# A decoder layer on one core: a pair of value units in 512 columns, the last product in two column halves, and an opening with x in quarters

## Chip, core, metric

The kernel runs on one core of a Trainium2 chip. The metric is device microseconds of one execution. The engines are PE (TensorE: matmuls, with PEld its weight loads), ACT (ScalarE), DVE (VectorE), POOL (GpSimd) and SP, whose queue issues nearly every DMA.

## What is computed

One decoder layer on 256 tokens of width 1024 with a memory of 256 tokens, and a final RMSNorm, all in float32. RWKV-7 has 8 heads of 64, attention 8 heads of 64, cross attention 4 heads of 256.

```python
def reference(x, mem, ...):
    u = rms_norm(h, norm_mix[l]); z = u @ w_in[l]
    y_rwkv = rwkv7_time_mix(z[..., :RWKV_IN], ...)
    y_moba = moba_attention(q, k, v)
    h = h + jnp.concatenate([y_rwkv, y_moba], axis=-1) @ w_mix_out[l]
    h = h + memory_cross_attention(rms_norm(h, ...), rms_norm(mem, ...), w_xq[l], w_xkv[l], w_xo[l])
    a = jnp.square(jax.nn.relu(rms_norm(h, norm_ffn[l]) @ w_ff1[l]))
    h = h + a @ w_ff2[l]
    return rms_norm(h, norm_final)
```

## The kernel before

**Units, halves, quarters.** All dense products are cut into units of 1 MB of weights (`UNITS`). In their order these are seven `z` (input projection of RWKV, units 0 to 6), four `mq` and two `mv` (queries, keys and values of the attention), four `xk` and three `xv` (keys and values of the memory, units 13 to 19), four `mix`, the last `xv`, four `xq`, four `xo`, then `f1` and `f2` (the MLP). SP loads unit u into one of three buffers of `raw`, once the unit three before it has been split. A unit has two halves `s`; `hi(s)` on ACT (L1081) rounds a half of `raw` into `w_hi`, `lo(s)` on DVE (L1589) writes the rest into `w_lo`, and PE multiplies hi by hi, hi by lo and lo by hi. The matmuls of a half come in two quarters, in the order of `QUARTERS`; a quarter has 12 matmuls of 256 columns, or 6 of 512. `dense(n)` in PE's program runs the next n quarters, in the text called q0, q1, ...

**Results.** `take(o)` on DVE scales output o out of a bank and counts `out_taken`. PE begins output o only when o-2 has been taken, since two banks (`dense_bank`) alternate. An `xv` unit gives 256 columns of the value matrix for both token halves, side by side in one bank: L465 to L467.

**The order** of each engine's program is written out by hand, as lists of calls such as `dense(2)`, `spread(0)`, `take(3)`. There is no scheduler. What waits, waits in that order.

**The opening.** SP loads the row `norm_mix`, then x in two halves of 512 columns (`x_in`) alternating with the halves of unit 0 (`first_in`), then 12 small parameter rows (L332), and unit 1. PE turns x, 256 columns per `load(0, q)` (L579, four transposes). ACT scales that into `op_hi` (L1133) and DVE makes `op_lo` (L1697). `copies` (L1705) keeps x for the residual. `stats(0)` on ACT (L1146) sums the squares of x for the norm, `diagonal_of(0)` on DVE makes a diagonal of it, and `spread(0)` on PE (L590) spreads it over a bank, from which `spread_copy` takes it. `params(1)` turns the parameter rows on PE (L562) and copies them on DVE (L1680 to L1684); `spread(0)` writes the bank from which that copy reads, and so waits for its end (`dve_params`).

**The middle.** `lora()` (L616) needs `gates()` of ACT. Then `rates()` on ACT, the scan `sums()` on DVE, `key_sums()`, `key_norm()`, `keys()`, and `tokens()` on PE (L663), which needs DVE's last product of the key chain (L1788).

**The end.** The last `f2` unit (columns 512 to 1023) runs token half 0, then token half 1, each as 12 matmuls of 512 columns. `finish()` takes four pieces, (token half, column half) = (0,0), (1,0), (0,1), (1,1). DVE adds the residual (L1996) and multiplies the gain (L1999). ACT sums the squares (L1298). After a token half's second piece come a root on ACT (L1304), a reciprocal on DVE (L2005), and the scaling by it, half of the columns on ACT (L1309) and half on DVE (L2008). SP then issues two stores per token half (L348).

## Time and profile before

| | |
|---|---|
| three timed runs | 471.09, 471.23, 471.69 us, median 471.23 |
| the profiled execution, its own time | 471.15 us |
| its span, first to last instruction | 469.3 us |
| busy share of PE, DVE, ACT, POOL | 97%, 69%, 50%, 7% |
| the chain that ended last, share on PE | 92% |

The profiled execution's own time lies 1.85 us over its span; what is found in the trace is a part of the span. The chain that ended last is followed back from the last instruction. As long as it stands on PE, only PE's own work sets the time.

### The profile page before, as it was taken

To read this page: it belongs to the slowest core of one execution; us is meant where nothing else is said; L and a number is where in the kernel's file an instruction comes from. 1 tells how busy PE (TensorE), PEld (TensorE's weight loads), DVE (VectorE), ACT (ScalarE), POOL (GpSimd) and SP (SyncE) were. 2 spreads that over 40 slices of the span, in tenths; PEclk is the share of its full clock that TensorE was granted. 3 is DMA by queue.
4 is the path that set the end of the run, shared out by engine and by line. 5 is a ranking of instruction groups with operands and counts; after the bars stand their busy time and mean duration, and the time that the engine had idled before them with its cause. 6 is when DMAs were issued, how large, how long until landed. Compare 5 with 4: busy or idle time off the path is not lost.

```text
span 469.3 us, 10580 instructions
## 1 busy us (share of the span) xinstructions
PE 454.7 (97%) x4518; PEld 413.7 (88%) x4518; DVE 323.6 (69%) x491; ACT 236.8 (50%) x373; POOL 34.8 (7%) x50
## 2 busy tenths in 40 slices
PE   5999999989999999999999999999999999999994
PEld 4999999979898899999998898888888888888883
DVE  4778999897576477668766368866555756574745
ACT  5789843343354226436444455545465546354534
POOL 8100000000000000071000001340000000000000
PEclk9999999999999999999999999999999999999999
DMA  7973534505060522462552166655656565856502
GB/s 255 336 239 94 180 112 157 185 9 176 3 205 5 178 92 91 134 226 91 180 179 91 33 189 189 218 180 180 180 153 207 186 199 163 260 181 217 184 0 91
DMA packets 61410, 73.07 MB, mean 156 GB/s; under 512 B 1314, under 2 KB 51572, under 8 KB 61364
## 3 DMA queue, kind: packets, MB, share of 16 engines
q1 hardware_dynamic: 61284, 72.14, 48.5%
q8 instruction: 36, 0.59, 0.5%
q0 software_dynamic: 80, 0.26, 0.2%
q14 instruction: 10, 0.08, 0.1%
HBM read 71.35 MB, written 1.05 MB: 154 GB/s over the span
## 4 chain that ended last, share of the span: by engine, by line
PE 92%; DVE 4%; DMA 1%; ACT 1%; issue 1%; SPq 0%; ACTq 0%
PE bank L497 13%; PE bank L512 11%; PE bank L513 10%; PE bank L514 10%; PE bank L529 6%; PE bank L531 6%; PE bank L530 6%; PE bank L499 6%; PE bank L465 2%; PE bank L466 2%; PE bank L467 2%; PE bank L881 2%; PE bank L905 1%; DMA xval<-in_x 1%; PE bank L641 1%; PE bank L496 1%
## 5 line engine op out<-in xcount | busy, mean ns | idle before, releaser
L1589 DVE TENSOR_TENSOR w_lo<-raw,w_hi 128x1024 fp32r<-128x1024 f32 x130 | 160.4, 1241 | 67.4 <-ACT w_hi L1081 67.1
L1081 ACT ACTIVATE w_hi<-raw 128x1024 fp32r<-128x1024 f32 x130 | 136.8, 1057 | 111.3 <-PE bank L514 52.0
L497 PE MATMUL bank<-op,w_hi 128*128 128x512 f32 x256 | 89.1, 398 | 0.0
L512 PE MATMUL bank<-op,w_hi 128*128 128x256 f32 x288 | 83.7, 291 | 0.1
L513 PE MATMUL bank<-op,w_hi 128*128 128x256 f32 x288 | 81.4, 283 | 0.1
L514 PE MATMUL bank<-op,w_lo 128*128 128x256 f32 x288 | 81.4, 283 | 0.0
L499 PE MATMUL bank<-op,w_lo 128*128 128x256 f32 x224 | 62.8, 281 | 0.0
L512 PEld LDWEIGHTS bank<-op,w_hi 128*128 128x128 f32 x288 | 55.1, 191 | 1.2 <-issue 0.8
L513 PEld LDWEIGHTS bank<-op,w_hi 128*128 128x128 f32 x288 | 55.2, 192 | 0.2
L514 PEld LDWEIGHTS bank<-op,w_lo 128*128 128x128 f32 x288 | 55.1, 191 | 0.2 <-issue 0.2
L497 PEld LDWEIGHTS bank<-op,w_hi 128*128 128x128 f32 x256 | 46.4, 188 | 8.8
L529 PE MATMUL bank<-w_hi,op_hi 128*128 128x512 f32 x128 | 50.0, 390 | 0.0
L531 PE MATMUL bank<-w_hi,op_lo 128*128 128x512 f32 x128 | 49.8, 389 | 0.0
L530 PE MATMUL bank<-w_lo,op_hi 128*128 128x512 f32 x128 | 49.8, 389 | 0.0
L499 PEld LDWEIGHTS bank<-op,w_lo 128*128 128x128 f32 x224 | 42.3, 189 | 1.3
L512 PE MATMUL bank<-op_hi,w_hi 128*128 128x256 f32 x128 | 37.9, 296 | 0.7 <-DVE op_lo L1984 0.7
L513 PE MATMUL bank<-op_lo,w_hi 128*128 128x256 f32 x128 | 36.2, 283 | 0.0
L514 PE MATMUL bank<-op_hi,w_lo 128*128 128x256 f32 x128 | 36.1, 282 | 0.0
L1114 ACT ACTIVATE tmp<-bank 128x256 f32<-128x256 f32 x32 | 12.3, 384 | 37.6 <-PE bank L497 37.5
L531 PEld LDWEIGHTS bank<-w_hi,op_lo 128*128 128x128 f32 x128 | 24.0, 188 | 5.1
L530 PEld LDWEIGHTS bank<-w_lo,op_hi 128*128 128x128 f32 x128 | 24.0, 188 | 5.0
L529 PEld LDWEIGHTS bank<-w_hi,op_hi 128*128 128x128 f32 x128 | 24.0, 188 | 4.7
(268 smaller groups left out, 732.1 us busy)
## 6 DMA issues: line engine op xcount, KB each, us to landing
raw<-in_w_ff SPq DMA_DIRECT2D x32, 1024.0 KB, 5.3
raw<-in_w_in SPq DMA_DIRECT2D x12, 1024.0 KB, 6.0
raw<-in_w_xkv SPq DMA_DIRECT2D x8, 1024.0 KB, 5.6
raw<-in_w_mix_out SPq DMA_DIRECT2D x4, 1024.0 KB, 5.1
raw<-in_w_xq SPq DMA_DIRECT2D x4, 1024.0 KB, 5.2
raw<-in_w_xo SPq DMA_DIRECT2D x4, 1024.0 KB, 5.4
xval<-in_x SPq DMA_DIRECT2D x2, 512.0 KB, 4.4
raw<-in_w_in SPq DMA_DIRECT2D x2, 512.0 KB, 5.4
```

The lines of the kernel that those rows point to most:

```text
L465: mm(dst, hi, wh[:, k, :], start=(xk == 0), stop=False)
L497: last = mm(b[:, :], wh[:, k, :], op_both[0][:, :, k, :], start=first, stop=final)
L499: mm(b[:, 0:T], wl[:, k, :], op_hi[0][:, k, :], start=False, stop=False)
L512: mm(dst, wh[:, k, :], op_hi[which][:, k, :], start=first, stop=False)
L513: mm(dst, wh[:, k, :], op_lo[which][:, k, :], start=False, stop=False)
L514: last = mm(dst, wl[:, k, :], op_hi[which][:, k, :], start=False, stop=final)
L529: mm(dst[:, :], hi, wh[:, k, :], start=first, stop=False)
L530: mm(dst[:, :], hi, wl[:, k, :], start=False, stop=False)
L531: last = mm(dst[:, :], lo, wh[:, k, :], start=False, stop=final)
L1081: op(view(w_hi), r, ACT.Copy).then_inc(hi_done, 1)
L1114: op(tmp[:, n % 2, T * half:T * half + T], half_bank(s)[:, T:2 * T], ACT.Copy).then_inc(act_part, 1)
L1589: tt(view(w_lo), r, view(w_hi).bitcast(f32), ALU.subtract).then_inc(lo_done, 1)
```

## The change

1. **Values in 512 columns.** Units 17 and 18 (`xv` 0 and 1) become one product of 512 columns: unit 17 holds input rows 0 to 511, unit 18 rows 512 to 1023, of the same 512 columns. Token half 0 goes to one bank, token half 1 to the other, which `o = 16` has to leave first; so `take(16)` stands earlier in DVE's list (before `state(3)`), and `take(17)` later (behind `pair_scores(3)`).
2. **The end.** For token half 1 the last unit is done in columns 512 to 767, then 768 to 1023, into another bank (`dense_bank[0]`). `finish()` has five pieces, and token half 1 is scaled 384 columns on ACT and 640 on DVE; ACT issues the store of its own part.
3. **The opening.** x comes in quarters, the second one ahead of unit 0's first half. `norm_mix` is issued by ACT. Unit 1 is issued ahead of the 12 parameter rows. PE runs transposes of `ident` into an unused bank (`warm`, 4 and 7 of them). The lists of calls are in another order.

```diff
-    out += [("xv", "w_xkv", 0, D + 256 * j, j) for j in range(3)]
+    out += [("xv", "w_xkv", 4 * j, D, j) for j in range(2)]
+    out += [("xv", "w_xkv", 0, D + 256 * j, j) for j in range(2, 3)]
     out += [("mix", "w_mix_out", 0, 256 * j, j) for j in range(4)]
...
+def wide_of(u):
+
+    what, _, _, _, j = UNITS[u]
+    return  what == "xv" and j < 2
...
                      ((0, 0), (2, 0), (0, 1), (1, 0), (1, 1), (2, 1), (3, 0), (3, 1))]
+    elif wide_of(_u) and UNITS[_u][4] % 2 == 0:
+
```
```diff
         gain_out, hid_sq = flat(s0[:, :, :]), flat(s3[:, :, :]).rearrange("p (n c) -> p n c", n=2)
-        fin = sb("fin", [128, 10])
-        r_sq, sq_sum, first_sum, root = fin[:, 0:2], fin[:, 2:6], fin[:, 6:8], fin[:, 8:10]
+        fin = sb("fin", [128, 12])
+        r_sq, sq_sum, first_sum, root = fin[:, 0:2], fin[:, 2:7], fin[:, 7:10], fin[:, 10:12]
+        PIECES = [(0, 0, 512), (1, 0, 512), (0, 512, 512), (1, 512, 256), (1, 768, 256)]
+        SIDE = [512, 384]
 
         bank = [ctx.enter_context(nc.psum_tensor(f"bank{i}", [128, 512], f32)) for i in range(8)]
...
             for half in range(2):
-                c, k = slice(512 * half, 512 * half + 512), slice(4 * half, 4 * half + 4)
-                sp.dma_start(stage[0][:, :, c], x[:, :, c]).then_inc(x_in[half], 16)
+                for q in (2 * half, 2 * half + 1):
+                    c = slice(256 * q, 256 * q + 256)
+                    sp.dma_start(stage[0][:, :, c], x[:, :, c]).then_inc(x_in[q], 16)
+                k = slice(4 * half, 4 * half + 4)
                 sp.dma_start(first_to[:, k, :], first[:, k, UNITS[0][3]:UNITS[0][3] + 256]).then_inc(first_in[half], 16)
...
-                k, n = (4, 512) if what == "f2" else (8, 256)
+                k, n = (4, 512) if what == "f2" or wide_of(u) else (8, 256)
                 sp.dma_start(raw[:, u % NRAW, :].rearrange("p (k c) -> p k c", k=k),
                              w[:, r:r + k, c:c + n]).then_inc(raw_in[u % NRAW], 16)
 
+            load_unit(1)
...
-            load_unit(1)
...
-            for n in range(NT):
-                for j, done in enumerate((act_final, dve_final)):
-                    c = slice(512 * j, 512 * j + 512)
-                    sp.wait_ge(done, n + 1)
-                    sp.dma_start(o[:, n, c], ostage[:, n, c]).then_inc(out_done, 16)
+            for n, done, c in ((0, act_final, slice(0, SIDE[0])), (0, dve_final, slice(SIDE[0], D)),
+                               (1, dve_final, slice(SIDE[1], D))):
+                sp.wait_ge(done, n + 1)
+                sp.dma_start(o[:, n, c], ostage[:, n, c]).then_inc(out_done, 16)
```
```diff
+                if wide_of(s // 2):
+                    j = UNITS[s // 2][4] % 2
+                    o -= j
+                    if j == 0 and q == BEGUN[s] + 1 and s == OUTS[o][1]:
+                        pe.wait_ge(out_taken, o)
+                    for k in range(2):
+                        xk = 4 * j + 2 * (s % 2) + k
+                        hi, lo = op_hi[which][:, xk, tokens_of(part)], op_lo[which][:, xk, tokens_of(part)]
+                        dst = dense_bank[(o + part) % 2][:, :]
+                        mm(dst, hi, wh[:, k, :], start=(xk == 0), stop=False)
+                        mm(dst, hi, wl[:, k, :], start=False, stop=False)
+                        last = mm(dst, lo, wh[:, k, :], start=False, stop=(xk == KT - 1))
+                    if q == DONE[s]:
+                        last.then_inc(dense_mm, 1)
+                    elif j and s % 2:
+                        last.then_inc(wide_mm, 1)
+                    return
                 if what in ("mv", "xv"):
 
...
                 dst = out_acc[n][j // 2]
+                if s // 2 == len(UNITS) - 1 and n == 1:
+                    c = slice(256 * i, 256 * i + 256)
+                    to = dense_bank[0][:, 0:256] if i else dst[:, c]
+                    if i == 1:
+                        pe.wait_ge(dve_add, 2 * len(KIND["f1"]))
+                    for k in range(4):
+                        xk = 4 * (g % 2) + k
+                        _, view = split_views(s - i + k // 2)
+                        hi, lo = op_hi[1][:, xk, tokens_of(n)], op_lo[1][:, xk, tokens_of(n)]
+                        mm(to, hi, view(w_hi)[:, k % 2, c], start=(i == 1 and k == 0), stop=False)
+                        mm(to, hi, view(w_lo)[:, k % 2, c], start=False, stop=False)
+                        last = mm(to, lo, view(w_hi)[:, k % 2, c], start=False, stop=(k == 3))
+                    last.then_inc(pe_acc, 1)
+                    return
                 for k in range(2):
                     xk = 4 * (g % 2) + 2 * i + k
```
```diff
+            def warm(n):
+
+                for _ in range(n):
+                    turn_op(dense_bank[1][:, 0:128], ident[:, :], ident[:, :])
+
...
-                    pe.wait_ge(x_in[q // 2], 16)
+                    pe.wait_ge(x_in[q], 16)
...
             params(0)
+            warm(4)
             load(0, 0)
             load(0, 1)
+            warm(7)
             load(0, 2)
             load(0, 3)
+            dense(3)
+            params(1)
+            dense(1)
+            spread(0)
+            dense(9)
+            lora()
+            dense(5)
+            key_sums()
+            dense(1)
+            spread(1)
+            dense(1)
+            keys(0)
+            dense(3)
+            load(1, 0)
             dense(2)
-            params(1)
-            dense(2)
-            spread(0)
-            dense(10)
-            lora()
-            dense(2)
-            spread(1)
-            dense(2)
-            key_sums()
-            dense(2)
-            keys(0)
-            dense(2)
-            load(1, 0)
             load(1, 1)
-            dense(12)
+            dense(9)
             tokens()
...
+            def opening():
+                act.dma_start(prow[0:8, :], io["norm_mix"].rearrange("l (r p) -> (l r) p", p=128)).then_inc(mix_in, 16)
+                act.wait_ge(pool_const, 1)
+                op(small[:, 15:16], eps[:, 0:1], ACT.Sqrt)
```
```diff
                     act.wait_ge(dve_hinv, n + 1)
                     act.wait_ge(dve_hgain, n + 1)
-                    out_half = ostage[:, n, 0:512]
-                    op(out_half, out_half, ACT.Copy, scale=root[:, n:n + 1]).then_inc(act_final, 1)
-
+                    out_part = ostage[:, n, 0:SIDE[n]]
+                    op(out_part, out_part, ACT.Copy, scale=root[:, n:n + 1]).then_inc(act_final, 1)
+                act.wait_ge(act_final, 2)
+                act.dma_start(out.rearrange("b (n p) d -> p (b n) d", p=128)[:, 1, 0:SIDE[1]],
+                              ostage[:, 1, 0:SIDE[1]]).then_inc(out_done, 16)
+
+            opening()
             load(0, 0)
             load(0, 1)
```
```diff
+                if wide_of(OUTS[o][0]):
+                    if j % 2:
+                        dve.wait_ge(dense_mm, OUTS[o][2] + 1)
+                    else:
+                        dve.wait_ge(wide_mm, wide_no(o))
+                    values_of, m = (mval, 0) if what == "mv" else (xval, 1)
+                    n = j % 2
+                    ts(values_of[:, n, 512 * (j // 2):512 * (j // 2) + 512], dense_bank[o % 2][:, :],
+                       row_sum[:, 2 * m + n:2 * m + n + 1], None, ALU.mult).then_inc(out_taken, 1)
+                    return
                 dve.wait_ge(dense_mm, OUTS[o][2] + 1)
...
                     dve.wait_ge(pe_acc, i + 1)
-                    h = h_tok[:, n, c]
-                    stt(out=h, in0=out_acc[n][j][:, :], scalar=r_sq[:, n:n + 1], in1=h, op0=ALU.mult, op1=ALU.add)\
-                        .then_inc(dve_h, 1)
+                    h = h_tok[:, n, c:c + 512] if c < 768 else h_tok[:, n, 768:D]
+                    src = out_acc[n][c // 512][:, :] if c < 768 else dense_bank[0][:, 0:256]
+                    stt(out=h, in0=src, scalar=r_sq[:, n:n + 1], in1=h, op0=ALU.mult, op1=ALU.add).then_inc(dve_h, 1)
+                    h = h_tok[:, n, c:c + size]
                     dve.wait_ge(dve_h, i + 1)
-                    tt(ostage[:, n, c], h, gain_out[:, c], ALU.mult).then_inc(dve_hgain, 1)
-                    if j == 0:
+                    tt(ostage[:, n, c:c + size], h, gain_out[:, c:c + size], ALU.mult).then_inc(dve_hgain, 1)
+                    if c + size < D:
                         dve.wait_ge(act_hsum, i + 1)
-                        ts(first_sum[:, n:n + 1], sq_sum[:, i:i + 1], 1.0 / D, NORM_EPS, ALU.mult, ALU.add).then_inc(dve_hsum, 1)
+                        if c:
+                            dve.wait_ge(dve_hsum, 2)
+                        ts(first_sum[:, (0, 1, 0, 2)[i]:(0, 1, 0, 2)[i] + 1], sq_sum[:, i:i + 1], 1.0 / D,
```

The rest of DVE's list up to `take(5)`, after, reads: `copies(0)`, `copies(1)`, `take(0)`, `lo(4)`, `follow(0)`, `take(1)`, `lo(5)`, `lo(6)`, `follow(1)`, `take(2)`, `diagonal_of(1)`, `lo(7)`, `follow(2)`, `lo(8)`, `sums()`, `take(3)`, `lo(9)`, `key_norm()`, `follow(3)`, `lo(10)`, `key_root()`, `lo(11)`, `spread_copy(1)`, `take(4)`, `keys(0)`, `lo(12)`, `follow(4)`, `keys(1)`, `lo(13)`, `take(5)`.

**PE, the opening.** PE's first instructions of before, with the semaphores that each waits for in brackets (`xval` holds x here, `op` the split x, `w_hi` the rounded weights):

```order
1 L558 MATMUL bank<-ident,prob 128x8 [waits mix_in,pool_const]
2 L579 MATMUL bank<-ident,xval 128x128 [waits x_in0]
3 L579 MATMUL bank<-ident,xval 128x128 x3
4 L579 MATMUL bank<-ident,xval 128x128 [waits x_in0]
5 L579 MATMUL bank<-ident,xval 128x128 x3
6 L579 MATMUL bank<-ident,xval 128x128 [waits x_in1]
7 L579 MATMUL bank<-ident,xval 128x128 x3
8 L579 MATMUL bank<-ident,xval 128x128 [waits x_in1]
9 L579 MATMUL bank<-ident,xval 128x128 x3
10 L478 MATMUL bank<-op,w_hi 128x256 [waits dve_op,hi_done]
```

And of the changed kernel, in its own line numbers; L618 is `warm`, L635 `load(0, q)`:

```order
1 L609 MATMUL bank<-ident,prob 128x8 [waits mix_in,pool_const]
2 L618 MATMUL bank<-ident 128x128 x4
3 L635 MATMUL bank<-ident,xval 128x128 [waits x_in0]
4 L635 MATMUL bank<-ident,xval 128x128 x3
5 L635 MATMUL bank<-ident,xval 128x128 [waits x_in1]
6 L635 MATMUL bank<-ident,xval 128x128 x3
7 L618 MATMUL bank<-ident 128x128 x7
8 L635 MATMUL bank<-ident,xval 128x128 [waits x_in2]
9 L635 MATMUL bank<-ident,xval 128x128 x3
10 L635 MATMUL bank<-ident,xval 128x128 [waits x_in3]
11 L635 MATMUL bank<-ident,xval 128x128 x3
12 L515 MATMUL bank<-op,w_hi 128x256 [waits dve_op,hi_done]
```

The turning of x waits for four loads instead of two, and 11 transposes of `ident` stand ahead of and in it.

**DVE, the opening.** From `lo(1)` to `spread_copy(0)` before; `w_lo` with `hi_done` is `lo`, the three rows from `par<-bank` on are `params(1)`:

```order
12 L1589 TENSOR_TENSOR w_lo<-raw,w_hi 128x1024 [waits hi_done]
13 L1711 RECIPROCAL row_sum<-row_sum 128x2 [waits act_root]
14 L1713 TENSOR_SCALAR prob<-ident,row_sum 128x128 [waits dve_link]
15 L1713 TENSOR_SCALAR prob<-ident,row_sum 128x128
16 L1680 COPY par<-bank 128x74 [waits pe_params]
17 L1682 TENSOR_SCALAR onemu<-par 128x14 [waits dve_link]
18 L1684 TENSOR_SCALAR one_k_a<-par 128x4
19 L1589 TENSOR_TENSOR w_lo<-raw,w_hi 128x1024 [waits hi_done,dve_params]
20 L1589 TENSOR_TENSOR w_lo<-raw,w_hi 128x1024 [waits hi_done]
21 L1718 COPY rinv<-bank 128x256 [waits pe_spread_rms]
```

And after:

```order
11 L1654 TENSOR_TENSOR w_lo<-raw,w_hi 128x1024 [waits hi_done]
12 L1786 RECIPROCAL row_sum<-row_sum 128x2 [waits act_root]
13 L1788 TENSOR_SCALAR prob<-ident,row_sum 128x128 [waits dve_link]
14 L1788 TENSOR_SCALAR prob<-ident,row_sum 128x128
15 L1654 TENSOR_TENSOR w_lo<-raw,w_hi 128x1024 [waits hi_done]
16 L1755 COPY par<-bank 128x74 [waits pe_params]
17 L1757 TENSOR_SCALAR onemu<-par 128x14 [waits dve_link]
18 L1759 TENSOR_SCALAR one_k_a<-par 128x4
19 L1654 TENSOR_TENSOR w_lo<-raw,w_hi 128x1024 [waits hi_done,dve_params]
20 L1793 COPY rinv<-bank 128x256 [waits pe_spread_rms]
21 L1780 COPY hT<-bank 128x512 [waits act_op] x4
```

`lo(2)` now stands ahead of `params(1)`, and one `lo` behind it.

**DVE, the end.** The second piece of token half 0 and the end of the program, before (L1996 residual, L1999 gain, L2005 reciprocal, L2008 scaling):

```order
425 L1996 SCALAR_TENSOR_TENSOR xval<-bank,fin,xval 128x512 [waits pe_acc]
426 L1999 TENSOR_TENSOR xkey<-xval,s 128x512 [waits dve_h]
427 L2005 RECIPROCAL fin<-fin 128x1 [waits act_hroot]
428 L2008 TENSOR_SCALAR xkey<-xkey,fin 128x512 [waits dve_hgain,dve_hinv]
429 L1996 SCALAR_TENSOR_TENSOR xval<-bank,fin,xval 128x512 [waits pe_acc]
430 L1999 TENSOR_TENSOR xkey<-xval,s 128x512 [waits dve_h]
431 L2005 RECIPROCAL fin<-fin 128x1 [waits act_hroot]
432 L2008 TENSOR_SCALAR xkey<-xkey,fin 128x512 [waits dve_hgain,dve_hinv]
```

After; L2071 is the residual, L2074 the gain, L2079 the sum of the earlier pieces' squares, L2086 the scaling:

```order
422 L2071 SCALAR_TENSOR_TENSOR xval<-bank,fin,xval 128x512 [waits pe_acc]
423 L2074 TENSOR_TENSOR xkey<-xval,s 128x512 [waits dve_h]
424 L2083 RECIPROCAL fin<-fin 128x1 [waits act_hroot]
425 L2086 TENSOR_SCALAR xkey<-xkey,fin 128x512 [waits dve_hgain,dve_hinv]
426 L2071 SCALAR_TENSOR_TENSOR xval<-bank,fin,xval 128x512 [waits pe_acc]
427 L2074 TENSOR_TENSOR xkey<-xval,s 128x256 [waits dve_h]
428 L2079 TENSOR_SCALAR fin<-fin 128x1 [waits dve_hsum,act_hsum]
429 L2071 SCALAR_TENSOR_TENSOR xval<-bank,fin,xval 128x256 [waits pe_acc]
430 L2074 TENSOR_TENSOR xkey<-xval,s 128x256 [waits dve_h]
431 L2083 RECIPROCAL fin<-fin 128x1 [waits act_hroot]
432 L2086 TENSOR_SCALAR xkey<-xkey,fin 128x640 [waits dve_hgain,dve_hinv]
```

Behind the scaling of token half 0 there are now two pieces, with three more instructions between them, where there was one.

## Rows read from the trace of the kernel before

**Rows 1.** The page: the span, and the chain that ended last by engine.
```profile
span 469.3 us, 10580 instructions
...
PE 92%; DVE 4%; DMA 1%; ACT 1%; issue 1%; SPq 0%; ACTq 0%
```

**Rows 2.** The chain of waits, 0 to 18 us: start us, us, what.
```profile
7.67 1.97 PE bank L579 x8
...
10.71 0.21 PE bank L479
...
11.09 0.12 PE bank L479
...
16.11 0.44 PE bank L590 x4
...
16.62 0.36 PE bank L512
```

**Rows 3.** The timeline, 0 to 32 us: start, duration, engine, line, [idle before <- releaser].
```profile
0.80 0.40 SPq L307 DMA_DIRECT2D prob<-in_norm_mix  x1
...
1.26 0.42 SPq L313 DMA_DIRECT2D xval<-in_x  x1
...
5.86 1.69 ACT L1133 ACTIVATE op<-bank,par 128x256 fp32r<-128x256 f32 x4 [3.56 <-PE bank L579]
...
7.44 1.06 ACT L1081 ACTIVATE w_hi<-raw 128x1024 fp32r<-128x1024 f32 x1
...
8.83 1.69 ACT L1133 ACTIVATE op<-bank,par 128x256 fp32r<-128x256 f32 x4 [0.33 <-PE bank L579]
...
14.65 0.22 DVE L1680 COPY par<-bank 128x74 f32<-128x74 f32 x1
...
15.25 2.36 DVE L1589 TENSOR_TENSOR w_lo<-raw,w_hi 128x1024 fp32r<-128x1024 f32 x2
```

**Rows 4.** The two loads of x, by tile.
```profile
DMA to landing us min/median/max: 3.4/4.4/5.4
```

**Rows 5.** The timeline of DVE, 52 to 67 us.
```profile
52.78 0.69 DVE L1633 TENSOR_TENSOR tmp<-bank,rinv 128x512 f32<-128x512 f32 x1 [0.45 <-PE bank L514]
...
65.56 1.22 DVE L1788 TENSOR_TENSOR s<-s,pend 128x1024 f32<-128x1024 f32 x1
```

**Rows 6.** The chain of waits, 66 to 80 us.
```profile
67.14 1.75 PE bank L663 x16
```

**Rows 7.** The timeline of PE in one quarter of an `xv` unit, 256 columns.
```profile
157.53 0.28 PE L466 MATMUL bank<-w_lo,op_hi 128*128 128x256 f32 x1
...
158.72 0.28 PE L467 MATMUL bank<-w_hi,op_lo 128*128 128x256 f32 x1
```

**Rows 8.** The timeline of PE in an `f2` unit, 512 columns.
```profile
445.01 0.39 PE L531 MATMUL bank<-w_hi,op_lo 128*128 128x512 f32 x1
...
445.69 0.39 PE L531 MATMUL bank<-w_hi,op_lo 128*128 128x512 f32 x1
```

**Rows 9.** The timeline from 457 us to the end.
```profile
458.86 0.74 DVE L1996 SCALAR_TENSOR_TENSOR xval<-bank,fin,xval 128x512 f32<-128x512 f32 x1
...
460.46 0.74 DVE L1996 SCALAR_TENSOR_TENSOR xval<-bank,fin,xval 128x512 f32<-128x512 f32 x1
...
462.52 0.49 DVE L2008 TENSOR_SCALAR xkey<-xkey,fin 128x512 f32<-128x512 f32 x1
...
465.18 0.72 ACT L1309 ACTIVATE xkey<-xkey,fin 128x512 f32<-128x512 f32 x1 [0.23 <-DVE fin L2005]
```

**Rows 10.** The timeline of SP's queue, the last issues.
```profile
465.93 0.81 SPq L348 DMA_DIRECT2D out<-xkey  x2
```

**Rows 11.** Groups of instructions by shape: count, busy us, mean ns of one.
```profile
L1091 ACT ACTIVATE zT<-tmp,onemu 128x256 f32<-128x256 f32 x14 | 6.3, 496 | 0.3 <-DVE tmp L1631 0.3
...
L1697 DVE SCALAR_TENSOR_TENSOR op<-bank,par,op 128x256 fp32r<-128x256 f32 x8 | 3.4, 474 | 4.0 <-ACT op L1133 4.0
```

73 lines of the change are left out of this document (37 added, 36 removed).

## Prediction

> **What bounds the kernel now.** The page first: the chain that ended last stands on PE for 92% of a span of 469.3 us [rows 1]. So a part of the change counts only by what it does to PE's path, or to the head and the tail where PE is not the last to be waited for. The chain of waits shows both. At the head the transposes of x start when the second half of x lands, at 7.67. A matmul of 256 columns then takes 0.21 us of the path until 10.7 and 0.12 from 11.1 on (PE's two clock levels, 1.2 and 2.4 GHz; before the rise PE had run the transposes from 7.67 on and seven matmuls), and unit 1's first matmul, q4, starts at 16.62 [rows 2]. From there PE runs nearly without a gap. The tail starts at 463.12 with DVE's residual of the last piece and goes through ACT and DVE by turns to SP's last issues at 465.93 [rows 9, 10].
>
> A sum is made against the profiled execution, 471.15 us by its own time, 0.08 under the median of the timed runs (471.23). What a measurement can tell from no change is about 0.2%, 0.94 us.
>
> **Opening: x earlier.** `norm_mix` leaves SP's queue, so x is issued 0.46 earlier (0.80 for 1.26) [rows 3]. The two halves of x landed 3.4 and 5.4 us after their issues at 1.26 and 2.23 [rows 3, 4] (the second at 7.63), with a half of unit 0 between them. That is two transfers of 512 KB in 2.97 us, 1.48 each. By this rate the quarters land at 3.5, 4.2, 6.4 and 7.2. PE's order in the changed kernel is row, four `warm`, `load(0,0)`, `load(0,1)`, seven `warm`, `load(0,2)`. Eight transposes took 1.97 [rows 2], some 0.21 each of the path while the clock is low. `load(0,0)` starts at 3.5, `load(0,1)` ends at 5.2, and seven more `warm` hold PE until 6.7 at the low clock, 6.4 if it has risen by then.
>
> ACT started `load(0,2)` at 8.83, 1.16 after its transposes began at 7.67 [rows 2, 3]; with four fast transposes that is 0.7. So ACT starts it at 7.2 (fast; before that ACT is busy from 4.65 on with `load(0,0)`, `load(0,1)` and `hi(0)`, which took 5.86 to 8.50 before) or 7.85 (slow). Everything behind it on ACT, `load(0,3)`, `hi(1)`, `stats(0)`, `hi(2)`, stands as before, and DVE's `lo(2)` follows it. So `lo(2)` comes earlier by 1.0 to 1.6. Between the two I take 1.3. `copies(0)`, moved back on DVE, was never on this path: DVE waits for ACT here.
>
> **Opening: one call later.** Now the order on DVE. `spread(0)` on PE waits for the end of `params(1)`, and that now stands behind `lo(2)`. Before, `lo(2)` started at 15.25 and ended at 16.43 (two in 2.36) [rows 3], and `spread(0)` had run beside it; q4 could start 0.2 later. After, behind the end of `lo(2)` come 0.60 for `params(1)` (14.65 to 15.25) [rows 3], then 0.51 for `spread(0)` (16.11 to 16.62) [rows 2], and two handovers of 0.05. q4 starts at 16.43 - 1.3 + 0.60 + 0.51 + 0.1 = 16.34 instead of 16.62: a gain of **0.28**, from 0.6 gained to nothing. PE, four quarters of 12 x 0.12 from 7.7 or 8.4 on, ends q3 near 13.4 to 14.5 and then stands still; the time that the faster start gave PE is lost there, and so the clock during q0 and q1 doesn't count.
>
> The parameter rows, now behind unit 1 (1 MB, landing near 11.6), are due at q2's end, near 12. Were they up to 2 us late they would still be ahead of `lo(2)`.
>
> **Opening: the rest of the lists.** `lora()` moves one quarter ahead, `keys(0)` and `load(1,1)` likewise around single quarters; PE's work up to `tokens()` is the same. What can grow is DVE's lag. DVE waited 0.45 for PE at 52.78 (`take(5)`), and then ran without a pause to the end of L1788 at 66.78 [rows 5], while PE began `tokens()` at 67.14 [rows 6]: a slack of 0.36. In the changed list `sums()` can start some 2 us earlier against q4, but `lo(9)` has moved behind it (1.2) and DVE then waits for the head sums on PE and for `hi(12)` on ACT, which stand where they stood. I estimate that DVE reaches `take(5)` 0.4 later against q4 than before, just the slack. I take a **loss of 0.1**, between 0 and 0.5.
>
> **Values in 512 columns.** The rows show 10 matmuls of 256 columns in 1.19 us, 0.119 each [rows 7], and 3 of 512 in 0.68, 0.227 each [rows 8]. 96 matmuls of 256 become 48 of 512: 48 x (0.238 - 0.227) = **0.54 gained**, all on PE's path, which the chain holds there. The added wait, of the second wide quarter for `take(16)`, is covered: `take(16)`, of 512 columns like the residual's 0.75 [rows 9], now stands right behind unit 16's end, and a quarter of 6 x 0.227 = 1.4 and a `state` step lie between. `take(17)` has two quarters and the head sums before its bank is wanted. If a transition or a wait does cost, I give it 0.25.
>
> **The end.** The chain of the last piece does shrink. A residual of 256 columns takes 0.47 instead of 0.75 [rows 9, 11]. ACT's time falls by 0.226 for 256 columns less (0.722 at 512, 0.496 at 256) [rows 9, 11], and I take the same for the squares. So from the residual's start to the scaling's start it is 2.06 (463.12 to 465.18) - 0.27 - 0.23 = 1.56. But DVE isn't free to start it. It scales token half 0 at 462.52 for 0.49 [rows 9], so to 462.95 or 463.0, and only then comes piece four, which was ready long before. Pieces follow each other on DVE at 1.60 (458.86 to 460.46) [rows 9], since DVE waits for ACT's squares; with 256 squares 1.37. The fifth piece starts at 462.95 + 1.37 = 464.32 where the fourth started at 463.12. Its scaling starts at 464.32 + 1.56 = 465.88, 0.70 later than 465.18. The scaling is 384 columns on ACT, 0.11 shorter. The two stores are issued beside each other instead of one after the other, the second 0.4 later (0.81 for both) [rows 10]: between nothing and 0.4 of that comes back, because the same 512 KB has to move, and I take 0.15. Sum 0.70 - 0.11 - 0.15 = **0.45 lost**, from 0.2 to 0.7. PE's two column halves cost 24 x 0.119 - 12 x 0.227 = 0.14, hidden beside DVE.
>
> On the stores the Trainium skill ("DMA: Bandwidth & Descriptors", section "Issuing engines are not separate DMA queues") says that issuing from several engines only saves the sequencer's time. By it the full 0.4 of SP's second issue would come back at most, and the end would lose 0.2.
>
> **Sum:** -0.28 + 0.1 - 0.54 + 0.45 = -0.27. 471.15 - 0.27 = 470.88, so **470.9 us**, no measurable change.
>
> **Rivals.**
>
> *The clock stays low in the opening.* `warm` is all transposes, and before, the clock was still low through the eight transposes from 7.67 on and rose only after some matmuls had run [rows 2]; the trace can't tell whether transposes raise it. If they don't, `load(0,2)` starts at 6.7, `lo(2)` gains 1.0, q4 gains nothing: 471.2. Chance 0.15. The Trainium skill ("TensorE: Matmul & The Clock Gate", Part 4, PE-mode transpose) says that transposes do not count as activity for the gate; by that rule this case would be sure.
>
> *`params(1)` costs nothing,* because `lo(2)` is done well before PE gets to `spread(0)`, say if PE is late in q0 to q3. Then q4 gains up to 1.3 and the time is 469.9. Against it stands that `hi(2)` follows `stats(0)` as before. Chance 0.12.
>
> *The tail pays as meant.* If DVE took the last piece at 463.25, right behind PE's end (463.1, when DVE now starts, + 0.14), its scaling would start at 464.81, 0.37 earlier, and the end would gain 0.37 + 0.11 + 0.15 = 0.63 instead of losing 0.45: 469.8. It would need DVE to have room for piece four ahead of 463.0; the rows show it scaling token half 0 until then. Chance 0.07.
>
> *Slower: DVE falls behind.* From `take(5)` on DVE has no pause for 14 us, and every microsecond that it comes later than the slack of 0.36 stops PE at `tokens()`. For the run to be slower by more than 0.94 the lag has to be over 1.6 where I find 0.4, for instance by `gates()` or `rates()` coming late to `lora()`. With a lag of 1.8: 472.2. Chance 0.11.
>
> The forecast keeps 0.55.
>
> **Numbers.** Inside the forecast the ends of the terms are -0.6 and 0, 0 and 0.5, -0.54 and -0.3, 0.2 and 0.7: 470.2 to 472.0 if all fell together. The two fast rivals stand at 469.8 and 469.9. The range 469.8 to 471.9 leaves out the slow rival and a part of the fast ones. Faster: the two fast rivals and a little of the forecast's edge, 0.23. Slower: 0.12. Same: 0.65.
>
> **What would show it.** Opening: PE idle for about 2 us ahead of `spread(0)`, ended by DVE's `params(1)`, and q4 near 16.3. Middle: `tokens()` less than 0.5 behind its place of before against q4. Values: 48 matmuls of 512 columns at 0.227. Tail: on DVE the residual of piece four starts when token half 0's scaling ends, not when PE is done, and the last scaling starts some 2.7 after PE's last matmul instead of 2.1. I am wrong if PE doesn't wait at `spread(0)`, if the squares or the sum of squares are quicker than these rows so that DVE is free earlier, or if a new wait shows between 16 and 100 us.

## The result and the profile after

The changed kernel takes 473.16 us (median of 13 runs), the kernel before beside it 471.73 (13 runs): ratio 1.0033, interval 1.0023 to 1.0044, so 1.1 to 2.1 us slower. The forecast was 470.9, with a range of 469.8 to 471.9. All times here are of executions at full clock but one: the profiled execution of e12_warm_only below took 745.08 us at a mean granted clock of 0.56, and of its trace only the DMA rate of the opening is used.

The page of the profiled execution (473.45 us by its own time), to compare with [rows 1]:

```profile
span 471.5 us, 10538 instructions
...
PE 88%; DVE 5%; ACT 3%; DMA 1%; issue 1%; SPq 0%; DVEq 0%; ACTq 0%
```

PE's share of the chain fell from 92 to 88%: ACT (1 to 3%) and DVE (4 to 5%) took its place, and the chain of the first 19 us says where (start us, us, what):

```profile
2.86 6.77 DMA xval<-in_x
...
9.67 1.13 PE bank L635 x4
...
10.82 0.35 ACT op L1194
...
11.55 1.05 ACT w_hi L1142
12.61 1.04 ACT neu L1207 x2
...
15.06 1.05 ACT w_hi L1142
...
16.14 1.23 DVE w_lo L1654
...
17.62 0.18 DVE one_k_a L1759
...
17.93 0.68 PE bank L646 x4
18.62 0.12 PE bank L549
```

The last quarter of x, issued at 2.86, lands at 9.6. Behind it stand, as before, the transposes, ACT's `load`, `hi(1)`, the statistics and `hi(2)`, then DVE's `lo(2)` at 16.14 (15.25 in [rows 3]), and behind `lo(2)` now `params(1)` and `spread(0)`. On PE's timeline unit 1 starts at 18.37, 1.75 later than in [rows 2]. SP's queue (start, duration):

```profile
0.81 0.95 SPq L333 DMA_DIRECT2D xval<-in_x  x2
...
2.31 1.02 SPq L333 DMA_DIRECT2D xval<-in_x  x2
...
3.88 0.51 SPq L345 DMA_DIRECT2D raw<-in_w_in  x1
4.43 3.79 SPq L354 DMA_DIRECT2D prob<-in_norm_mem  x1
```

The first parameter row behind unit 1 takes 3.79 to issue; before it took 0.43. And between 3.5 and 6.5 us the DMA engines move little, though 3 MB are queued by 4.4. The windows of PE of the changed kernel (us, PE busy, granted clock, DMA share, GB/s):

```profile
3.50:6.50 3.00, 3.00 (x17) 1.00 0.71 208
...
9.50:12.50 3.00, 2.90 (x14) 0.50 1.02 323
12.50:13.00 0.50, 0.50 (x4) 0.57 0.33 106
13.00:13.50 0.50, 0.50 (x6) 1.00 0.50 109
```

and the same stretch of the kernel before:

```profile
3.50:6.50 3.00, 1.79 (x8) 1.00 1.05 382
```

The windows also show the clock: after a wait of 2.16 for x, PE is granted half its clock (1.2 GHz) from 9.5 to about 12.9, and unit 0 begins in that stretch.

Two more places. On PE's timeline there is a wait that no engine releases ("issue"):

```profile
125.12 0.43 PE L919 MATMUL bank<-probT,mval 128*64 128x256 f32 x1
125.81 0.43 PE L919 MATMUL bank<-probT,mval 128*64 128x256 f32 x2 [0.27 <-issue]
```

And the end, the timeline of DVE and ACT, to compare with [rows 9]:

```profile
464.36 0.49 DVE L2086 TENSOR_SCALAR xkey<-xkey,fin 128x512 f32<-128x512 f32 x1
464.76 0.74 DVE L2071 SCALAR_TENSOR_TENSOR xval<-bank,fin,xval 128x512 f32<-128x512 f32 x1
...
466.21 0.47 DVE L2071 SCALAR_TENSOR_TENSOR xval<-bank,fin,xval 128x256 f32<-128x256 f32 x1
...
467.79 0.61 ACT L1370 ACTIVATE xkey<-xkey,fin 128x384 f32<-128x384 f32 x1 [0.23 <-DVE fin L2083]
468.43 0.39 ACTq L1372 DMA_DIRECT2D out<-xkey  x1
```

The same step before and after gives the ledger of the two profiles. A step's place counts against the kernel before: +1.75 at unit 1's first matmul, +1.97 at `tokens()` (68.95 for 66.98), +1.70 at 121, +2.38 from 127 on (the wait at 125), +2.15 at the first wide quarter (a wait of 0.27 that the kernel before had at 148.31 is gone), +1.81 behind unit 18, +2.61 at the last scaling, +2.2 at the end of the span.

### The profile page after: what moved, and what is told of

Its sections match the earlier page's. It is cut to its first block, busy times and chain, and to the rows that moved or that the text cites. A ratio compares the mean times of both kernels' runs of the same rounds, so it can differ in the third digit from the quotient of the medians.

```text
span 471.5 us, 10538 instructions
## 1 busy us (share of the span) xinstructions
PE 456.9 (97%) x4493; PEld 413.2 (88%) x4493; DVE 324.4 (69%) x492; ACT 236.5 (50%) x375; POOL 34.7 (7%) x50
## 4 chain that ended last, share of the span: by engine, by line
PE 88%; DVE 5%; ACT 3%; DMA 1%; issue 1%; SPq 0%; DVEq 0%; ACTq 0%
PE bank L534 13%; PE bank L549 11%; PE bank L550 10%; PE bank L551 10%; PE bank L580 6%; PE bank L582 6%; PE bank L581 6%; PE bank L536 6%; PE bank L937 2%; DMA xval<-in_x 1%; PE bank L502 1%; PE bank L503 1%; PE bank L504 1%; PE bank L961 1%; PE bank L697 1%
## 5 line engine op out<-in xcount | busy, mean ns | idle before, releaser
L580 PE MATMUL bank<-w_hi,op_hi 128*128 128x512 f32 x124 | 48.4, 390 | 0.0
L582 PE MATMUL bank<-w_hi,op_lo 128*128 128x512 f32 x124 | 48.3, 389 | 0.0
L581 PE MATMUL bank<-w_lo,op_hi 128*128 128x512 f32 x124 | 48.2, 389 | 0.0
```

Of the source, the lines that this page charges most:

```text
L580: mm(dst[:, :], hi, wh[:, k, :], start=first, stop=False)
L581: mm(dst[:, :], hi, wl[:, k, :], start=False, stop=False)
L582: last = mm(dst[:, :], lo, wh[:, k, :], start=False, stop=final)
```

## The experiments

Times are medians; a ratio is against runs of the kernel before on the same chip. "q4" is the start of unit 1's first matmul on PE's timeline; "segment" is PE's time from its first value product (L919) to the first matmul of `states_out()` that reads `neu` (L872), which the expectations call the first state step; the wide values, where present, save 0.17 in it.

### The three parts apart

**e1_values_only.** Only the units, `wide_of`, the wide branch of `dense`, `take` and the order of `take(16)` and `take(17)`:

```diff
+     out += [("xv", "w_xkv", 4 * j, D, j) for j in range(2)]
```

> The kernel before, with the value pair in 512 columns alone. Theory A (the terms of the sum stand by themselves): PE's work between the first wide quarter and the end of unit 17 is 0.34 us shorter, as in the trace of the changed kernel (0.54 by the prediction), and the time is 0.3 to 0.5 us below the kernel before; unit 1's first matmul stays near 16.6. Rival B (a wait for take(16) or take(17) eats it): PE shows a gap before a wide quarter and the time is that of before or above.

471.45 us, ratio 0.9995 (0.9984 to 1.0005). By the time alone nothing is decided; in the trace the stretch of the pair, units 17 and 18, is 0.34 to 0.36 shorter (0.15 to 0.17 ahead of `states_out()`, 0.19 behind) with no wait before a wide quarter. Theory A in the trace.

**e2_end_only.** Only `PIECES`, `SIDE`, the branch for the last `f2` unit and the stores.

> The kernel before, with the end in column halves and the last store issued by ACT alone. Theory A (DVE is the bound of the tail): DVE takes the fourth piece only after scaling token half 0, the fifth 1.4 to 1.5 us later, and the last scaling starts 0.7 to 0.8 us later than before; the time is 0.35 to 0.5 us above the kernel before. Rival B (the column halves pay as meant): the last scaling starts 0.4 us earlier and the time is 0.6 us below.

472.16 us, ratio 1.0015 (1.0006 to 1.0024): 0.3 to 1.1 slower. DVE's timeline:

```profile
463.53 0.74 DVE L2014 SCALAR_TENSOR_TENSOR xval<-bank,fin,xval 128x512 f32<-128x512 f32 x1
...
464.98 0.47 DVE L2014 SCALAR_TENSOR_TENSOR xval<-bank,fin,xval 128x256 f32<-128x256 f32 x1
...
466.56 0.55 DVE L2029 TENSOR_SCALAR xkey<-xkey,fin 128x640 f32<-128x640 f32 x1
```

The fifth piece follows the fourth by 1.45. Theory A.

**e3_opening_only.** Only the four lists, the queues, quarters and `warm`.

> The kernel before, with the changed opening alone (SP, ACT, PE and DVE lists, x in quarters, unit 1 ahead of the rows). Theory A (the opening carries the whole loss): the second pair of x quarters lands near 9 and 9.6, unit 1's first matmul starts at 18.0 to 18.5, and the time is 1.3 to 1.9 us above the kernel before. Rival B (the loss of the whole comes from the interplay, or from an instruction fetch that PE meets near 125 us): the time is within 0.6 us of the kernel before.

472.59 us, ratio 1.0021 (1.0011 to 1.0031), about 1.0 slower. q4 at 18.68, and PE's wait for nothing stands at 126.29 (0.41). The three ratios add to 1.0031, the whole has 1.0033: the parts stand by themselves. The opening gives most of the loss, though less than theory A's 1.3. In this trace DVE is not on the way to q4: from the second load's transposes (8.78) to q4 the chain stands on PE alone, at the slow pace (0.21 for 256 columns) until 15.0. The same holds in e6_no_warm and e7_params_first.

### Why x lands late

**e4_unit1_behind.**

```diff
-             load_unit(1)
              for name, (r, c) in ROW.items():
...
+             load_unit(1)
```

> The changed kernel, with unit 1 issued behind the parameter rows again. Theory U (1 MB of unit 1 in front is what holds up the second pair of x quarters and SP's queue): the long issue of the first row (3.8 us) is gone, x lands as a whole by 8.0, ACT's load(0,2) starts by 8.2, unit 1's first matmul at 16.3 to 17.0, and the time is 1.2 to 1.8 us below the changed kernel. Theory Q (quarters of 256 KB are slower transfers themselves): SP's long issue is gone but x's second pair still lands at 8.7 or later, and unit 1's first matmul stays above 17.7; the time is within 0.6 us of the changed kernel.

473.43 us, ratio 1.0033 (1.0020 to 1.0046). SP's long issue is gone and x's last quarter still takes 7.0 to land. By that my first theory, U, falls. The q4 of 19.07 and the time say nothing on x, which I had overlooked: the chain to q4 starts at unit 1, issued at 8.36 and landed at 15.4, on which `hi(2)` waits:

```profile
8.36 7.05 DMA raw<-in_w_in
15.43 1.07 ACT w_hi L1142
16.53 1.23 DVE w_lo L1654
```

**e5_x_halves.**

```diff
-                for q in (2 * half, 2 * half + 1):
-                    c = slice(256 * q, 256 * q + 256)
-                    sp.dma_start(stage[0][:, :, c], x[:, :, c]).then_inc(x_in[q], 16)
+                c = slice(512 * half, 512 * half + 512)
+                sp.dma_start(stage[0][:, :, c], x[:, :, c]).then_inc(x_in[half], 16)
```

> The changed kernel, with x in two transfers of 512 columns again, unit 1 still ahead of the rows. Theory Q (quarters are the slow part): x's second half lands by 7.8, ACT's load(0,2) starts by 8.2, SP's long issue of the first row stays, and unit 1's first matmul starts at 16.3 to 17.2: 1.0 to 1.8 us below the changed kernel. Theory U (unit 1 in front is the slow part): x's second half lands at 8.7 or later, and the time is within 0.6 us of the changed kernel.

472.76 us, ratio 1.0022 (1.0011 to 1.0033). The stretch from 3.5 to 6.5 moves 357 GB/s, x is in by 8.3, q4 at 17.36: 1.0 earlier than in the changed kernel. Of that about 0.5 shows in the time, and the intervals of the two kernels overlap. Theory Q for the mechanism; the size was less than expected.

**e8_halves_unit1.** Both edits.

> The changed kernel with x in halves and unit 1 behind the rows, so that of the new opening norm_mix on ACT's queue, warm and the new lists are left. Theories U and Q both: x is in by 7.3 (the kernel before had 7.63 with an issue 0.46 later), unit 1's first matmul starts at 15.9 to 16.5, and the time is 1.4 to 2.0 us below the changed kernel, near the kernel before or up to 0.4 us below it. Rival L (the lists themselves cost): x is in by 7.3 and the time still stays 0.5 us or more above the kernel before.

472.66 us, ratio 1.0022 (1.0011 to 1.0033), q4 at 17.28. x was issued 0.42 earlier than before and is in no earlier (8.2), which neither theory had. The time is as rival L has it, so something else costs too; in this trace a wait of 0.80 for nothing stands at 125.28.

**e9_token_rows.**

```diff
-                for q in (2 * half, 2 * half + 1):
-                    c = slice(256 * q, 256 * q + 256)
-                    sp.dma_start(stage[0][:, :, c], x[:, :, c]).then_inc(x_in[q], 16)
+                c = slice(512 * half, 512 * half + 512)
+                for n in range(2):
+                    sp.dma_start(stage[0][:, n, c], x[:, n, c]).then_inc(x_in[half], 16)
```

> The changed kernel, with x in four transfers of 256 KB that are cut by tokens instead of by columns, so that each still has rows of 2 KB as the halves had (each half of the columns is waited for as a whole). Theory R (the rows of 1 KB of the column quarters are what slows the stretch from 3.5 to 6.5 us): that stretch moves 290 to 400 GB/s, x is in by 8.3, unit 1's first matmul starts near 17.3, and the time is 0.3 to 0.9 us below the changed kernel. Theory N (the number or the size of the transfers slows it): the stretch stays at 120 to 280 GB/s and x is in at 9.0 or later, with the time of the changed kernel.

473.70 us, ratio 1.0045 (1.0032 to 1.0058). Windows of PE:

```profile
3.50:6.50 3.00, 2.33 (x12) 1.00 0.86 231
```

The last piece takes 7.3 to land. Rows of 2 KB are as slow as rows of 1 KB. Theory N, or something that belongs to x. The time, at the median 0.5 above the changed kernel, is not separated from it.

**e15_w0_quarters.** The kernel before with `for k in (slice(4 * half, 4 * half + 2), slice(4 * half + 2, 4 * half + 4))` around unit 0's transfer: also six transfers ahead of the rows.

> The kernel before, with each half of unit 0 in two transfers of 256 KB, x in halves as before. Theory M (more transfers of 256 KB in the queue at once slow the stretch from 3.5 to 6.5 us, whatever they carry): it moves 120 to 290 GB/s there instead of 320 to 390, and x's second half lands at 8.9 or later. Theory X (only the cut of x does it): 310 GB/s or more, x's second half in by 8.4.

471.58 us (one run). Windows of PE:

```profile
3.50:6.50 3.00, 1.56 (x8) 1.00 1.03 365
```

Theory X: the count of transfers is not it, only x's cut is. All twenty profiles divide so: six with x in four pieces move 207 to 242 GB/s between 3.5 and 6.5 us, fourteen with x in halves 319 to 382.

### What warm does

**e6_no_warm.** `warm(4)` and `warm(7)` out.

> The changed kernel without the eleven warm transposes. Theory A (the clock that warm raises has fallen again before the weights, since PE waits 2.2 us for x, so warm buys nothing): the granted clock during unit 0's quarters is no lower than with warm, the high clock comes by 12.9 or earlier, and the time is within 0.3 us of the changed kernel. Rival W (warm helps): unit 0's quarters run slow for longer and the time is above the changed kernel by 0.3 us or more. Rival V (warm hurts, by holding PE or lowering what is granted later): the time is below it by 0.3 us or more.

472.82 us, ratio 1.0024 (1.0014 to 1.0033), 0.3 to 0.4 under the changed kernel, which the intervals don't separate. I was wrong on the clock: a matmul of unit 0 goes at the slow pace (0.21) until 14.2 instead of 12.9. That `warm` does this isn't shown by the pair, since e3_opening_only has `warm` and is slow until 15.0. q4 is at 18.30 all the same. What I had not looked for: PE's wait for nothing has left 125 and stands at 149.95, near where the kernel before has it.

**e12_warm_only.** The kernel before and `warm`.

> The kernel before, with the eleven warm transposes and nothing else. Theory S: the wait for instructions appears at 123 to 128 us and costs 0.7 to 1.1 in the stretch from the first value product to the first state step (42.1 us without); unit 1's first matmul starts 0.3 to 0.9 us earlier; the time is within 0.5 us of the kernel before. Rival P (the place of that wait has another cause, the new lists): no wait near 125 us, and the time falls by what the opening gains, 0.5 us or more.

471.85 us, ratio 1.0009 (1.0000 to 1.0018). No gain, rather 0.4 lost. The place of the wait can't be read from its trace.

**e10_values_store.** The kernel before with the wide values and, at the end,

```diff
+        SIDE = [512, 384]
...
+                act.wait_ge(act_final, 2)
+                act.dma_start(out.rearrange("b (n p) d -> p (b n) d", p=128)[:, 1, 0:SIDE[1]],
+                              ostage[:, 1, 0:SIDE[1]]).then_inc(out_done, 16)
```

but the four pieces of before.

> The kernel before, with the value pair in 512 columns and the last store's ACT part (384 columns) issued by ACT; no column halves at the end and the opening of before. Theory A (terms as measured): values give 0.36, the store and the shorter scaling 0.24, no wait of PE for instructions near 125 us, and the time is 0.4 to 0.8 us below the kernel before. Rival B (the values' gain is lost in noise and the store is bounded by its transfer): within 0.2 us of the kernel before.

470.91 us, ratio 0.9986 (0.9976 to 0.9997): 0.1 to 1.1 below the kernel before, and below the changed kernel. No wait for nothing from 100 to 160 us, segment 41.89.

**e11_values_store_warm.** That kernel with `opening()` on ACT and `warm`.

> The kernel of the run before, with norm_mix on ACT's queue and the eleven warm transposes, but x in halves, unit 1 behind the rows and the lists of before (params(1) ahead of lo(2)). Theory S (warm moves where PE waits for its instructions, and costs there about what it gives in the opening): the eight transposes of x's second half take 1.1, unit 1's first matmul starts at 16.3 to 16.8 (0.5 to 0.9 earlier), a wait for instructions stands at 124 to 128 us and PE takes 0.7 to 1.1 longer between the first value product and the first state step; the time is within 0.4 us of the run before. Rival G (warm is a gain): the time is 0.5 us or more below that run.

471.43 us, ratio 0.9996 (0.9987 to 1.0005), 0.5 above, with overlapping intervals. A wait of 0.41 at 124.78, segment 42.82, q4 17.48 against 16.66. The cost came as theory S has it, the gain did not: the eight transposes took 1.97, not 1.1.

**e13_tiny_count.** e10_values_store with, between `load(0, 1)` and `load(0, 2)`,

```diff
+            for _ in range(11):
+                turn_op(dense_bank[1][0:8, 0:8], ident[0:8, 0:8], ident[0:8, 0:8])
```

> The kernel before with the values in 512 columns and the last store's part on ACT (470.91 us as it ran alone), and eleven transposes of 8 by 8 in PE's wait for x's second half: as many instructions as warm, next to no work. Theory C (the count of PE's instructions ahead decides where it waits for instructions): a wait for instructions appears at 123 to 128 us, the stretch from the first value product to the first state step is 42.4 to 43.0 instead of 41.9, and the time is 0.4 to 1.0 us above 470.9. Rival D (what warm does to the clock or the opening's timing is the cause): that stretch stays within 0.2 of 41.9 and the time within 0.3 us of 470.9.

472.36 us, ratio 1.0010 (0.9999 to 1.0022). PE's waits, 100 to 160 us, here and then in e10_values_store:

```profile
PE bank L898 <- issue: 0.4, 1, 0.4
PE bank L500 <- DVE w_lo L1629: 0.3, 1, 0.3
```

```profile
PE bank L500 <- DVE w_lo L1627: 0.3, 1, 0.3
```

The wait is at 124.51 and the segment 42.49, 0.60 above e10_values_store, as theory C has it. Eight columns each are next to no work, so it is their number that moves the wait. By the ratios the time is 1.1 above e10_values_store, more than the segment explains: q4 too is 0.39 later (17.05 for 16.66), though x was in early (7.58), with PE at the slow pace through the whole of q0. What PE may wait for is in the DMA view of the changed kernel, 124 to 130 us:

```profile
q8 instruction: 1, 0.02, 1.4%
```

The program's instructions come in transfers of 16 KB. In DMA views of 1 us of the changed kernel one moves at 123.6 us and the next at 128.7; the wait lies between them, at 125.5, behind 156 matmuls, nearly all small, and 154 weight loads in the 3 us from 122. The other traces show the same pattern. In all fourteen with such a wait, early or late, it ends 2.2 to 2.8 us behind an instruction transfer. In the nine with the wait at 124 to 129 the next transfer comes 2.8 to 2.9 behind its end, 5.1 to 5.7 behind the one before; in seven without a wait there (before, e1, e2, e6, e10, e14, e17) the two stand 4.3 to 4.4 apart. So the transfers keep step with PE's program. That eleven instructions ahead move the wait is shown; that PE waits for the instructions themselves is argued from this, since no transfer ends in the wait.

### The lists

**e7_params_first.** DVE's `lo(2)` behind `params(1)` again.

> The changed kernel with DVE's params(1) ahead of lo(2), as before the change. Theory A (the order on DVE costs what the prediction said, one call of 0.60 in the way of spread(0)): PE's wait ahead of spread(0) goes, unit 1's first matmul starts 0.3 to 0.7 us earlier, and the time falls by as much. Rival B (the parameter rows, issued up to 11.7, land too late for DVE to take them ahead of lo(2), or PE's own quarters are the bound): the first matmul of unit 1 moves by less than 0.2 us.

472.83 us, ratio 1.0020 (1.0009 to 1.0031). The wait ahead of `spread(0)` is gone and q4 0.29 earlier. The time is 0.3 to 0.6 lower, which the intervals don't separate. From x's transposes (8.94) to q4 the chain stands on PE alone.

**e14_lists_alone.** x in halves, unit 1 behind, no `warm`.

> The changed kernel with x in halves, unit 1 behind the rows and without warm: of the opening only norm_mix on ACT's queue and the new lists are left, beside the values and the end. By the terms as measured (values -0.36, end +0.55 to +0.7, opening: the order params(1) behind lo(2) 0 to +0.6, no wait near 125 us): 471.7 to 472.6, 0.0 to 0.8 above the kernel before. Theory C: no wait for instructions at 123 to 128 us. If the lists cost more than the order on DVE, the time is 472.7 or above.

472.16 us, ratio 1.0007 (0.9998 to 1.0016). No wait near 125 (theory C again). On PE:

```profile
17.52 0.68 PE L644 MATMUL bank<-prob,ones 128*128 128x128 f32 x4 [1.14 <-DVE one_k_a L1755]
17.96 0.36 PE L547 MATMUL bank<-op,w_hi 128*128 128x256 f32 x1
```

PE waits 1.14 for `params(1)`. `lo(2)` itself follows unit 1 here, which was issued at 7.68 and landed at 14.6, and not x. q4 comes 2.24 after the start of `lo(2)` (15.72), where before it was 1.37 (15.25 to 16.62).

**e18_lists_params_first.** The same with `params(1)` ahead.

> The run e14_lists_alone (472.16 us, 0.33 above before) with DVE's params(1) ahead of lo(2) again. Theory A (params(1) behind lo(2) sets unit 1's first matmul, since spread(0) waited 1.14 for it there): PE's wait ahead of spread(0) goes or falls below 0.2, that matmul starts 0.7 to 1.1 earlier against lo(2)'s start, and the time falls by 0.4 to 1.0 us. Rival B (lo(2), now later by 0.6, holds unit 1 instead): the matmul gains less than 0.4 and the time less than 0.3 us.

471.97 us, ratio 1.0008 (0.9998 to 1.0018). The wait is gone and q4 is 1.37 after `lo(2)`; but in that profile x came 0.6 later (8.70) and q4 stands at 17.75. In the time nothing is left of it (0.2 at the median): rival B's number. The order on DVE costs as computed against `lo(2)`; what it costs the kernel stays below what can be measured.

**e17_best_with_lists.** That kernel with the end of e10_values_store.

> The same as the other kernel of this call, with the end of before and only the last store's 384 columns on ACT: values, store and new lists together. If the terms add (column halves at the end cost 0.79 at the last scaling): 0.6 to 1.0 us below the other kernel of this call, and 470.4 to 471.2. If the lists cost something of their own, it is above 471.2, behind the kernel with the lists of before (470.91).

471.58 us, ratio 0.9996 (0.9987 to 1.0004). That is 0.4 below e18_lists_params_first at the median, where 0.6 to 1.0 was expected, and 0.5 above e10_values_store by the ratios, with overlapping intervals: the new lists and norm_mix on ACT bring no gain that can be measured. The last scaling stands 2.49 behind PE's last matmul here and 3.00 in e18_lists_params_first.

**e16_x_first.** e10_values_store with both halves of x ahead of unit 0 and all four `load` calls ahead of `hi(0)` and `lo(0)`.

> The kernel before with the values in 512 columns and the last store's part on ACT (470.91 us), with both halves of x issued ahead of unit 0, and ACT and DVE taking all four load calls ahead of hi(0) and lo(0). Theory F (x is what the opening waits for): x is in by 6.8, the statistics end 0.5 to 1.0 earlier, unit 1's first matmul starts at 15.9 to 16.4, and the time is 0.3 to 0.8 us below 470.9. Rival H (unit 0 then lands too late, and hi(0) or the first quarter takes the place of the wait): unit 1's first matmul at 16.6 or later, and the time within 0.3 us of 470.9 or above.

473.57 us, ratio 1.0038 (1.0025 to 1.0052), q4 at 19.62. x is in early, and PE waits for the weights:

```profile
4.82 3.68 PE L616 MATMUL bank<-ident,xval 128*128 128x128 f32 x16 [2.25 <-DMA xval<-in_x]
10.98 0.58 PE L515 MATMUL bank<-op,w_hi 128*128 128x256 f32 x1 [2.48 <-ACT w_hi L1118]
```

Rival H.

The openings side by side, without e16_x_first and e12_warm_only:

| opening | second load of x transposed from | q4, lowest to highest (mean) |
|---|---|---|
| halves, norm_mix on SP (before, e1, e2, e10, e13, e15) | 7.58 to 8.38 | 16.62 to 17.99 (17.14) |
| halves, norm_mix on ACT (e5, e8, e11, e14, e17, e18) | 8.10 to 8.70 | 17.28 to 18.47 (17.72) |
| x in four (after, e3, e4, e6, e7, e9) | 8.58 to 10.07 | 18.08 to 19.63 (18.69) |

In e4_unit1_behind and e14_lists_alone unit 1 sets q4 and not x. In the traces where the chain runs on PE alone from x's transposes to q4, q4 comes 8.9 to 10.2 behind their start, and the difference is how long the slow pace lasts. The kernel before in the profile that I predicted from had the earliest q4 of all. And the segment, with 0.17 added where the values are wide: 41.8 to 42.1 in five profiles without such a wait (e1, e2, e10, e14, e17); 42.4 to 42.6 in five with one at 148 to 152 (before, e6, e15, e16, e18); 42.7 to 43.4 in all nine that have eleven more transposes (after, e3, e4, e5, e7, e8, e9, e11, e13), each with the wait at 124 to 129.

## Why the prediction was wrong

**Opening, the arrival of x: this step failed.** "That is two transfers of 512 KB in 2.97 us, 1.48 each. By this rate the quarters land at 3.5, 4.2, 6.4 and 7.2." The first two were in time (the eight transposes of `load(0,0)` and `load(0,1)` run at 3.80 without a wait); the third came at 8.9 and the last at 9.6. I took a rate from two large transfers and laid it on four small ones. So `lo(2)`, for which I had 1.3 earlier, came 0.89 later: a term mis-sized by 2.2 against the profile of before. By the runs, the cut of x moves q4 by 1.0 (e5, e8 against after), and the time by about 0.5 at the median, which the intervals don't separate. The rest of the miss on x is that the gain didn't exist: x issued 0.45 earlier, in halves, is in no earlier.

**The sum of the miss.** By the ratios of e1, e2 and e3 the values gave 0.2, the end cost 0.7 and the opening with its lists 1.0, where the sum had -0.54, +0.45 and -0.18. So of the 1.7 to 1.8 by which the change came out worse, about 1.2 is the opening. Another 0.6 of the distance from 470.9 to 473.16 is the base: the one profile stood at 471.15, the median of 13 runs at 471.73.

**Opening, one call later: right, and small.** PE did wait for `params(1)`, 0.30 in the changed kernel, where it was late itself, and 1.14 in e14_lists_alone. By my sum q4 stands 16.34 - 13.95 = 2.39 behind the start of `lo(2)`, where before it was 1.37; measured 2.23 and, in e14_lists_alone, 2.24. That "the clock during q0 and q1 doesn't count" was wrong: with x late, PE reached `spread(0)` only 0.30 ahead of DVE, and a slow clock to 12.9 had used up the slack. In e3, e6 and e7 PE doesn't wait there at all, and the pace of q0 and q1 sets q4 by itself.

**The clock rival.** In e8_halves_unit1 the pace rose with nothing but transposes run (start, us):

```profile
6.05 1.70 PE L616 MATMUL bank<-ident 128*128 128x128 f32 x7
8.29 1.10 PE L633 MATMUL bank<-ident,xval 128*128 128x128 f32 x8 [0.54 <-DMA xval<-in_x]
```

Eight transposes took 1.10 there, 1.97 before [rows 2]. The rule of the Trainium skill ("TensorE: Matmul & The Clock Gate", Part 4, PE-mode transpose), that they don't count, does not hold here; the measurement decides. But the gain is not to be had reliably: with the same `warm` the eight took 1.97 in e11, and after a wait of 2.16 in the changed kernel 1.87, at a clock that then fell.

**What was missing: PE's instructions.** No term of mine had the wait at 125. In the profiled pair it took 0.68, less 0.23 for the one at 148 that went. By the segments, eleven more transposes ahead cost 0.7 (mean 42.92 over nine profiles against 42.22 over ten), at 128 columns as at 8. What `warm` gains in the opening isn't reliable and this cost is there each time, which is why it doesn't pay.

**The lag at `tokens()`:** predicted 0.1 (0 to 0.5), measured 0.22, and given back by 121 us. **Values:** predicted 0.54, measured 0.34 to 0.36. [Rows 8] gave 0.227 for a matmul of 512 columns; on PE's timeline of the changed kernel ten of them take 2.32:

```profile
175.55 0.40 PE L489 MATMUL bank<-w_lo,op_hi 128*128 128x512 f32 x1
...
177.87 0.39 PE L490 MATMUL bank<-w_hi,op_lo 128*128 128x512 f32 x1
```

At 0.232 the product is 48 x (0.238 - 0.232) = 0.29: a price taken from another unit was 0.005 too low, which is half the gain when two nearly equal numbers are subtracted. **The end:** predicted 0.45, with the last scaling 0.70 later and 0.26 given back; in the profiles 0.80 and 0.41, in e2_end_only 0.7 (0.3 to 1.1). The steps on DVE came as written: the fourth piece right behind token half 0's scaling, the fifth 1.45 later (1.37 predicted). The last scaling started 2.7 behind PE's end, for 2.1 before, as the prediction had it. The store issued by ACT and the shorter scaling gave back 0.41 in this pair, mean 0.22 over the profiles; in e10_values_store they are kept without the column halves. The Trainium skill ("DMA: Bandwidth & Descriptors", "Issuing engines are not separate DMA queues") says that a second issuing engine saves only the time of issuing. The traces agree: 0.41 is less than the 0.4 of SP's second issue and the 0.11 of the scaling together.

## What to carry to other kernels

A rate read from a few large transfers need not hold for smaller ones at the start; cut a load on the critical path only if a profile of the cut shows its landing. Instructions that seem free, put where an engine waits, still count as instructions: ahead of a burst of small matmuls they moved, here, the point where PE stopped. And where one profile is the base of a sum in tenths, its opening should be compared with a second one: here unit 1 started anywhere from 16.6 to 18.0 in kernels with the same opening.

## What the runs showed that was not expected

- x in four pieces lowers the early DMA rate by a third (207 to 242 GB/s, mean 222, for 319 to 382, mean 350), by columns or by tokens, with or without unit 1 behind; unit 0 in four pieces does not (365). Why stays open.
- Behind 1 MB in front, SP's issue of a 4 KB row takes 3.79 (1.77 with x in halves, 0.57 with unit 1 behind). Without it x lands no earlier (e4); what it costs otherwise no run shows, since unit 1 lands late there.
- PE waits, probably for its own instructions, 0.2 to 0.8 in a record and up to 1.4 on the path. Eleven transposes of 8 by 8, over a hundred microseconds earlier, move that wait from 149 or nowhere to 125. Why there, stays open.
- The slow pace of PE ended at 10.8 in the kernel before and at 13.9 in e2_end_only with the same opening, while the records granted 1.00 in both.
